# A gated recurrence on one core: two pairs of PSUM banks for the level products, the next keys prepared a level ahead, and a shorter norm chain

## What is computed

```python
def chunked_gated_recurrence(q, k, v, log_f):
    ...
    def step(state, inp):
        qc, kc, vc, lfc = inp
        b = jnp.cumsum(lfc, axis=2)
        ...
        scores = jnp.einsum('nhtk,nhsk,nhtsk->nhts', qc, kc, decay)
        o_intra = jnp.einsum('nhts,nhsv->nhtv', scores, vc)
        ...
def hgrn2_mixer(x, w_in, lower_bound, norm_g, w_out):
    q, f_fw, f_bw, i_in, g = jnp.split(x @ w_in, 5, axis=-1)
    ...
    o = o[:bsz] + flip(o[bsz:])
    o = rms_norm(o, norm_g)
    ...
    o = o * jax.nn.silu(g)
    return o @ w_out
```

## Time and profile before

| what | value |
| --- | --- |
| median of three runs | 2890.19 us (2887.98 to 2890.64) |
| profiled execution, its own time | 2895.3 us |
| its span in the profile | 2893.5 us |
| TensorE busy, share of the span | 2668.3 us, 92% |
| VectorE busy, share | 1422.0 us, 49% |
| ScalarE busy, share | 555.3 us, 19% |
| GpSimd busy, share | 618.9 us, 21% |
| mean granted TensorE clock | 0.959 of full speed |

### The profile page before, as it was taken

How to read it: one execution, slowest core, us unless ns; L and a number is a source line. 1 busy time by engine, 2 the same in 40 slices (tenths; PEclk the granted TensorE clock), 3 DMA queues, 4 the chain that set the end, 5 groups by cost and what they waited for, 6 DMA issues and landing times. The chain is left out here.

```text
span 2893.5 us, 35029 instructions
## 1 busy us (share of the span) xinstructions
PE 2668.3 (92%) x13476; PEld 2229.2 (77%) x13476; DVE 1422.0 (49%) x2579; ACT 555.3 (19%) x825; POOL 618.9 (21%) x448
## 2 busy tenths in 40 slices
PE   6786889999999999978999999995899999999996
PEld 5676678788888888767888888885778888888875
DVE  8699526523332232463666766666472232333227
ACT  3224232211111111012322222320211111111110
POOL 2969211111112111111111111100111111111210
PEclk8898899999999999989999999996999999999998
DMA  4333223121111111021011011100511112111101
GB/s 133 85 104 100 78 74 131 58 59 44 43 43 43 58 43 58 8 72 37 23 37 37 22 36 29 36 7 0 185 57 50 44 43 58 43 43 43 43 15 58
DMA packets 207701, 157.96 MB, mean 55 GB/s; under 512 B 15616, under 2 KB 189824, under 8 KB 206720
## 3 DMA queue, kind: packets, MB, share of 16 engines
q1 hardware_dynamic: 207616, 156.81, 17.8%
HBM read 139.02 MB, written 17.76 MB: 54 GB/s over the span
## 5 line engine op out<-in xcount | busy, mean ns | idle before, releaser
L588 DVE TENSOR_TENSOR h<-h,ps 128x512 f32<-128x512 f32 x320 | 219.6, 686 | 201.2 <-PE ps L365 200.9
L347 PE MATMUL ps<-aT_hi,w_hi 128*128 128x512 f32 x704 | 278.4, 395 | 3.2 <-DVE aT_lo L561 3.2
L347 PE MATMUL ps<-aT_hi,w_lo 128*128 128x512 f32 x704 | 276.6, 393 | 0.0
L347 PE MATMUL ps<-aT_lo,w_hi 128*128 128x512 f32 x704 | 274.4, 390 | 0.0
L1738 PE MATMUL ps<-aT_hi,w_hi 128*128 128x512 f32 x640 | 258.4, 404 | 1.7 <-PEq L241 1.7
L1738 PE MATMUL ps<-aT_hi,w_lo 128*128 128x512 f32 x640 | 251.6, 393 | 0.0
L1738 PE MATMUL ps<-aT_lo,w_hi 128*128 128x512 f32 x640 | 250.9, 392 | 0.0
L1710 POOL TENSOR_TENSOR w_lo<-w_raw,w_hi 128x1024 fp32r<-128x1024 f32 x38 | 93.0, 2454 | 578.2 <-ACT w_hi L62 578.2
L571 DVE TENSOR_TENSOR s5o_act_out<-s5o_act_out,ps 128x512 f32<-128x512 f32 x44 | 30.2, 687 | 351.5 <-ACT s5o_act_out L460 351.5
L571 DVE TENSOR_TENSOR hgo_act_out<-hgo_act_out,ps 128x512 f32<-128x512 f32 x44 | 30.2, 687 | 349.9 <-ACT hgo_act_out L460 349.9
L1771 PE MATMUL ps<-hg_q_decayed,hg_k_used 128*128 128x128 f32 x896 | 128.7, 302 | 34.7 <-DVE hg_scores L2062 31.9
(11 more groups left out here) (325 smaller groups left out, 5951.2 us busy)
## 6 DMA issues: line engine op xcount, KB each, us to landing
w_raw<-in_ffn_w_in_dram SPq DMA_DIRECT2D x44, 512.0 KB, 5.1
w_raw<-in_hg_w_in_dram SPq DMA_DIRECT2D x40, 512.0 KB, 3.9
s5o_raw<-in_ffn_w_in_dram SPq DMA_DIRECT2D x22, 512.0 KB, 5.0
s5o_raw<-in_ffn_w_out_dram SPq DMA_DIRECT2D x11, 1024.0 KB, 5.0
hgo_raw<-in_ffn_w_in_dram SPq DMA_DIRECT2D x22, 512.0 KB, 5.0
hgo_raw<-in_ffn_w_out_dram SPq DMA_DIRECT2D x11, 1024.0 KB, 5.0
h<-in_x_dram SPq DMA_DIRECT2D x4, 1024.0 KB, 9.0
s_w_raw<-in_s_w_in_dram SPq DMA_DIRECT2D x8, 512.0 KB, 4.9
```

The source lines that it names most:

```text
L347: ins = t.matmul(ps[:, 2 * b + a, :], w[q][:, a, kk, :], x[:, kk, rows], start=(kk == 0 and m == 0), stop=(kk == KT - 1 and m == 2))
L588: v.tensor_tensor(part, part, ps[:, 4 + m % 4, :], ALU.add).then_inc(S["out_acc"], 1)
```

## The change

It has five parts. Odd levels write banks 4 and 5 instead of 2 and 3, so a level waits for the scores of the level before the last (`level_kept` of `lv - 1`), and level 1 of a head waits for the former head's output to be out of banks 4 and 5 (`o_kept`) instead. `advance_k(n, lv)`, the step that brings k forward, now stands a level ahead: for level 0 of the next head it stands at the end of a head, behind `keep_g` ("behind the gate"), and for level `lv + 1` it stands behind the scores' copy of level `lv`. The diagonal scores are taken behind the q move of level 0 instead of ahead of everything. `turn_k` waits for level 5's scores instead of `o_kept`. The norm chain has three Newton steps of three operations instead of four of four, which makes 11 small operations with the mean instead of 18. With three Newton steps instead of four the inverse root is computed by a slightly different approximation.

```diff
--- before.py
+++ after.py
@@ -1629,7 +1629,7 @@
     OUTS = HG_OUTS
     BUF = [0, 1, 0, 1, 0]
     USES = [BUF.count(0), BUF.count(1)]
-    CORE = 2 * (NHC - 2) + 1 + RSQRT_STEPS
+    CORE = 2 * (NHC - 2) + 2 + 3 * NEWTON
     PREPARED = 2 * HLV + 2
 
     def first(n):
@@ -1766,16 +1766,18 @@
                         t.wait_ge(E["o_normed"], n)
                 if lv:
                     t.wait_ge(E["level_moved"], HLV * n + lv)
-                    t.wait_ge(E["level_kept"], HLV * n + lv)
+                if lv == 1 and not first(n):
+                    t.wait_ge(E["o_kept"], 2 * n)
+                if lv >= 2:
+                    t.wait_ge(E["level_kept"], HLV * n + lv - 1)
                 for c in range(NHC):
-                    ins = t.matmul(bank_rows(2)[:, c, :], k_used[lv % 2][:, c * HC:(c + 1) * HC], q_used(lv, c),
+                    ins = t.matmul(bank_rows(2 + 2 * (lv % 2))[:, c, :], k_used[lv % 2][:, c * HC:(c + 1) * HC], q_used(lv, c),
                                    start=True, stop=True)
                 ins.then_inc(E["level_done"], 1)
 
             def turn_k(n):
                 t.wait_ge(E["level_moved"], HLV * (n + 1))
-                if not first(n):
-                    t.wait_ge(E["o_kept"], 2 * n)
+                t.wait_ge(E["level_kept"], HLV * n + HLV - 1)
                 t.wait_ge(E["diag_kept"], n + 1)
                 for d in range(2):
                     for c in range(NHC):
@@ -2019,48 +2021,57 @@
                 for d in range(2):
                     v.tensor_tensor(Q[d][:, :], q_raw[:, :], f_raw[d][:, :], ALU.mult).then_inc(E["prepared"], 1)
 
+            def advance_k(n, lv):
+
+                now, then = k_used[lv % 2], k_used[1 - lv % 2]
+                if lv == HLV - 1:
+                    v.tensor_copy(halves(then, lv, 1), halves(k_other, lv, 1)).then_inc(E["k_passed"], 1)
+                else:
+                    passed = [a[:, :].rearrange("p (b e) -> p b e", e=4 << lv)[:, :, 1 << lv:3 << lv]
+                              for a in (then, k_other)]
+                    v.tensor_copy(*passed).then_inc(E["k_passed"], 1)
+                v.wait_ge(E["k_passed"], HLV * n + lv + 1)
+                carry(v, n)
+                for d in range(2):
+                    by = pair(d, lv, 1 - d)
+                    if lv == HLV - 1:
+                        v.tensor_tensor(halves(k_other if d else then, lv, d), halves(now, lv, d),
+                                        bc(by, 2, [P, NHC, 1 << lv]), ALU.mult)
+                    else:
+                        by = by.rearrange("p (b e) -> p b e", e=2)
+                        for e in range(2):
+                            v.tensor_tensor(quarter(then if d == e else k_other, lv, 2 * e + d),
+                                            quarter(now, lv, 2 * e + d),
+                                            bc(by[:, :, e], 2, [P, T // (4 << lv), 1 << lv]), ALU.mult)
+
             def core(n, more):
                 link = Steps(E["chain"], n * CORE)
                 v.wait_ge(E["prepared"], (n + 1) * PREPARED)
-                v.wait_ge(E["diag_done"], n + 1)
-                for b in range(2):
-                    ins = v.tensor_tensor(scores[:, 4 * b:4 * b + 4, :],
-                                          ps[:, 6 + b, :].rearrange("p (c t) -> p c t", t=HC),
-                                          bc(k.ident[:, :], 1, [P, 4, HC]), ALU.mult)
-                ins.then_inc(E["diag_kept"], 1)
-                v.wait_ge(E["diag_kept"], n + 1)
                 for lv in range(HLV):
-                    now, then = k_used[lv % 2], k_used[1 - lv % 2]
+                    v.wait_ge(E["level_done"], HLV * n + lv + 1)
+                    carry(v, n)
                     if not (first(n) and lv == 0):
                         v.wait_ge(E["level_moved"], HLV * n + lv)
                         carry(v, n)
-                    if lv == HLV - 1:
-                        v.tensor_copy(halves(then, lv, 1), halves(k_other, lv, 1)).then_inc(E["k_passed"], 1)
-                    else:
-                        passed = [a[:, :].rearrange("p (b e) -> p b e", e=4 << lv)[:, :, 1 << lv:3 << lv]
-                                  for a in (then, k_other)]
-                        v.tensor_copy(*passed).then_inc(E["k_passed"], 1)
-                    v.wait_ge(E["k_passed"], HLV * n + lv + 1)
-                    carry(v, n)
-                    for d in range(2):
-                        by = pair(d, lv, 1 - d)
-                        if lv == HLV - 1:
-                            v.tensor_tensor(halves(k_other if d else then, lv, d), halves(now, lv, d),
-                                            bc(by, 2, [P, NHC, 1 << lv]), ALU.mult)
-                        else:
-                            by = by.rearrange("p (b e) -> p b e", e=2)
-                            for e in range(2):
-                                v.tensor_tensor(quarter(then if d == e else k_other, lv, 2 * e + d),
-                                                quarter(now, lv, 2 * e + d),
-                                                bc(by[:, :, e], 2, [P, T // (4 << lv), 1 << lv]), ALU.mult)
-                    v.wait_ge(E["level_done"], HLV * n + lv + 1)
-                    carry(v, n)
                     for d in range(2):
                         qs = halves(Q[d], lv, 1 - d)
                         ins = v.tensor_tensor(qs, qs, bc(pair(d, lv, d), 2, [P, T // (2 << lv), 1 << lv]), ALU.mult)
                     ins.then_inc(E["level_moved"], 1)
-                    v.copy_predicated(scores[:, :, :], bc(mask[:, lv, :], 1, [P, NHC, HC]), bank_rows(2)
-                                      ).then_inc(E["level_kept"], 1)
+                    if lv == 0:
+                        v.wait_ge(E["diag_done"], n + 1)
+                        for b in range(2):
+                            ins = v.tensor_tensor(scores[:, 4 * b:4 * b + 4, :],
+                                                  ps[:, 6 + b, :].rearrange("p (c t) -> p c t", t=HC),
+                                                  bc(k.ident[:, :], 1, [P, 4, HC]), ALU.mult)
+                        ins.then_inc(E["diag_kept"], 1)
+                        v.wait_ge(E["diag_kept"], n + 1)
+                        carry(v, n)
+                    v.copy_predicated(scores[:, :, :], bc(mask[:, lv, :], 1, [P, NHC, HC]),
+                                      bank_rows(2 + 2 * (lv % 2))).then_inc(E["level_kept"], 1)
+                    if lv < HLV - 1:
+                        v.wait_ge(E["level_moved"], HLV * n + lv + 1)
+                        carry(v, n)
+                        advance_k(n, lv + 1)
                     if more and lv < 2:
                         keep_q(n + 1, lv)
 
@@ -2087,7 +2098,16 @@
                 v.wait_ge(E["o_squared"], NHC * (n + 1))
                 v.tensor_scalar(ms[:, :], ms[:, :], 1.0 / P, RMS_EPS, ALU.mult, ALU.add).then_inc(E["chain"], 1)
                 v.wait_ge(E["chain"], link.step())
-                rsqrt_steps(link, v, rs[:, :], rt[:, :], ms[:, :])
+                v.tensor_scalar(rs[:, :].bitcast(I32), ms[:, :].bitcast(I32), -0.5, 1597463007.0, ALU.mult, ALU.add
+                                ).then_inc(E["chain"], 1)
+                v.wait_ge(E["chain"], link.step())
+                for _ in range(NEWTON):
+                    v.tensor_tensor(rt[:, :], rs[:, :], rs[:, :], ALU.mult).then_inc(E["chain"], 1)
+                    v.wait_ge(E["chain"], link.step())
+                    v.scalar_tensor_tensor(rt[:, :], rt[:, :], -0.5, ms[:, :], ALU.mult, ALU.mult).then_inc(E["chain"], 1)
+                    v.wait_ge(E["chain"], link.step())
+                    v.scalar_tensor_tensor(rs[:, :], rt[:, :], 1.5, rs[:, :], ALU.add, ALU.mult).then_inc(E["chain"], 1)
+                    v.wait_ge(E["chain"], link.step())
                 for b in range(2):
                     ins = v.tensor_tensor(scores[:, 4 * b:4 * b + 4, :],
                                           ps[:, 2 + b, :].rearrange("p (c t) -> p c t", t=P),
@@ -2101,6 +2121,8 @@
                 if more:
                     for half in range(2):
                         keep_g(n + 1, half)
+                    v.wait_ge(E["init"], n + 2)
+                    advance_k(n + 1, 0)
                 assert link.n == CORE
 
             for half in range(2):
@@ -2109,6 +2131,8 @@
                 keep_g(0, half)
             prepare_totals(0)
             prepare_q(0)
+            v.wait_ge(E["init"], 1)
+            advance_k(0, 0)
             core(0, True)
             with v.Fori(1, HEADS - 1) as n:
                 core(n, True)
```

## The result

The changed kernel takes 2858.97 us (median of four runs, 2856.04 to 2860.54) against 2890.18 us for the kernel before (2887.98 to 2890.64). The ratio is 0.9889 (95% interval 0.9877 to 0.9902): 31.2 us faster, where 31.1 were forecast. The profiled execution took 2860.23 us, with a span of 2858.4 us.

The account below looks back on a forecast made before the run. TensorE was taken to bound the middle heads, with time winnable only where it stands still. Savings of 15.5 + 5.7 + 1.4 + 8.5 = 31.1 us from the median 2890.2 give 2859.1 us (-1.08%), range 2850 to 2870.

Parts of the forecast that it names:

- What a stall is worth: Each TensorE stall costs 0.25 us beyond its listed wait: 0.16 hidden idle time and about 0.09 for restarting.
- all thirteen of the levels' stalls: Two pairs of banks remove the scores-copy waits at levels 1 and 3 outside the last head: 15.5 us.
- five of the turning's: The shorter norm chain removes five of six TensorE waits before turning outputs: 4.6 us listed, 5.7 us in all.
- 81.7 us a head: Sign of being right: the middle heads lie 81.7 us apart instead of 85.3.
- Level 1's tight place: At head boundaries, level 1's q move arrives 0.1 us before it is wanted, so the stall goes without slack.
- three more operations held in turn: Feared at the boundary: GpSimd's subtractions (2.4 us each) hold k-step operations, making the q move 5 to 7 us late.
- The first rival: Level 1 of six heads keeps its 1.09 + 0.25 us stall: 8 us less gain, 2867 us; chance 0.13.
- the slower one: Rival: level 1 waits longer for the q move than for the copy; 11 us slower, 2901 us; chance 0.03.
- the 2.6 us of my step: In the last head, level 1 starts 2.6 us earlier, with diagonal operations and scores copy now behind it.
- The chain: Norm chain: eleven operations at 0.203 us take 2.24 us instead of 3.66; the last head gains 1.4 us in full.
- The last head: Its levels save 7.2 us at the low clock, 12.0 at the high; 8.5 us taken.
- VectorE's pace: In the last head at full clock, VectorE sets the distance of the levels at 4.3 us.

Follow-up runs that it names:

- e2: The kernel before with only the two pairs of banks and their waits, old order and old norm chain: 2866.53 us, ratio 0.9914.
- e1: The kernel before with only the shorter norm chain of three fused Newton steps: 2881.32 us, ratio 0.9967.
- e8: The kernel before once more, nothing edited, for a second profile: 2889.14 us, block 743.32 us.
- e3: The kernel before with the two pairs of banks and the short norm chain, in the old order of VectorE: 2863.70 us, ratio 0.9903.
- e7: The changed kernel once more, nothing edited, for a second profile: 2857.51 us, ratio 0.9882 against the kernel before.
- e6: The changed kernel with extra matmuls, read by nobody, where TensorE waits in head 7: 2853.46 us, ratio 0.9878 against the kernel before.
- e10: The changed kernel with e6's extra matmuls, and ScalarE taking the copy of each k step in head 7: 2849.88 us, ratio 0.9854 against the kernel before.
- e5: The changed kernel with the old norm chain of four Newton steps (18 small operations): 2869.47 us, ratio 0.9925 against the kernel before.
- e9: The changed kernel with a fourth fused Newton step in the norm chain: 2859.05 us, ratio 0.9884 against the kernel before.
- e4: The changed kernel with one pair of banks again, new order and short chain kept: 2887.76 us, ratio 0.9988 against the kernel before.
- e11: The same kernel as e6, run again beside e10: 2854.64 us, ratio 0.9868 against the kernel before.

## Why the prediction was right

*What a stall is worth, and all thirteen of the levels' stalls, with five of the turning's.* 15.5 + 5.7 = 21.2 us were forecast; heads 0 to 6 gave 1.2 + 19.9 = 21.1. e2 and e1 show that each part takes its own waits: 2.33 us of a middle head by the banks (85.28 to 82.95) and 1.01 by the chain, which makes 3.34, where both together gave 3.32. The turning's price, 0.92 + 0.22 = 1.14 us in five heads, was right: e1 gives 1.12 to 1.17 in each. Left out were the 0.3 us that heads 0 and 6 gain without a listed wait, 0.6 in all. The levels were priced too high by about as much: 2.50 us a head where e2 gives 2.33, so that a level's stall costs some 0.20 us beyond what is listed (14.0 us gained in heads 1 to 6 of e2, 11.6 listed in e8, twelve stalls) and not 0.25. That the two cancel is luck. The forecast of 81.7 us a head took the price of a head with all three stalls from a mean that includes head 6, which has only two; it is 81.95.

*Level 1's tight place.* The reckoning, a copy held by GpSimd until 0.29 us behind its subtractions, four free multiplications and a q move 0.1 us before it is wanted, came out within a tenth: 0.28, and 0.14 us. The Trainium skill, SBUF — State Buffer, "Who interferes with whom", says that the second to start is blocked on the shared port; the trace agrees for the copy (1.95 us against 0.43 in e3, where it comes at the end of GpSimd's work). What the rule made me fear, three more operations held in turn, did not happen, since the pair of subtractions had ended. The first rival (level 1 keeps its stall) and the slower one fall with that.

*What I credited to the order.* Nothing in the sum hung on it in the middle heads, but the text reads as if the place of the k step were needed there. e3 shows that it is not. It starts level 1 of head 7 1.2 us earlier; the other 1.3 of the 2.6 us of my step came from the banks, since in e3, too, level 1 no longer waits for the scores copy. The block of e7 is 3.7 us below e3's, but little of that can be put down to the order. 2.7 lie ahead of head 1: 1.35 before the first level 0, where e3's first 10 us ran at a granted clock of 0.85 and e7's at 1.00, and 1.4 in head 0, which takes 83.5 us in e6 and e10 too, and they have the new order. The other 1.0 lies in the levels of head 7, which scatter by as much (e5 and e9, with the new order and the same levels as e7, took 36.01 and 36.05 against 34.76). The medians of e3 and the changed kernel differ by 4.7 us, and their intervals (0.9888 to 0.9919, 0.9877 to 0.9902) overlap.

*The chain.* The fused operation on 128x8 was taken at 0.203 us and is 0.20 from start to start. The forecast chain of 2.24 us is 2.21. In the last head I gave it 1.4 us, and the wait ahead of the turning there shows just that: 8.22 or 8.23 us in the four kernels with the old chain (before, e8, e2, e5) and 6.78 to 6.80 in five with the new one (changed, e7, e1, e3, e4). The whole stretch behind the levels gains 1.5 us by e8 and e7, 1.6 by e1, but 0.9 by e3 against e2 and 0.2 by e7 against e5, since the work ahead of that wait scatters: from the turning of k to the first output 9.2 to 10.6 us, the outputs themselves 6.6 to 8.0, in instructions that these edits leave alone.

*The last head.* The term that was mis-sized most: 8.5 forecast, 10.1 measured (44.90 to 34.76). The frame was right, 7.2 at the low clock and 12.0 at the high. I took a value near the row with 0.51, but with the shorter stands (idle times of TensorE between two levels) the clock came back for part of the levels (0.71 in the window, two levels of 2.05 us among four of 3.04 to 3.78). e6 shows the cause: with nothing changed but added work on TensorE the clock is 0.95 and the levels lie 4.23 us apart, VectorE's pace (4.3 forecast). The Trainium skill, TensorE: Matmul & The Clock Gate, "What's actually happening", has activity release the throttled clock; the trace agrees, in part in the changed kernel (0.71) and fully in e10 (1.00). Against the block's 32.8 us the sum of 31.1 is short by 1.7, and 1.6 of that is this term. The two comparisons of medians give 31.2 and 33.0 us, so that the first meets the forecast within 0.1 is luck.

## What to carry to other kernels

Where two engines hand over through one buffer, ask which of the waits a second buffer removes and what is late next: here the second pair of banks was worth 24 us of 31, the shorter chain 7 to 8, and the rewritten order 1.2 us that can be located. An operation that reads PSUM can run in the time in which GpSimd works beside VectorE (the diagonal took its usual 1.28 us there in e3), while a copy from SBUF to SBUF is held (1.95 us in place of 0.43); so move the copy out of that time, if something useful can take its place, and count first, for here it was a draw. A stretch in which TensorE waits again and again is priced at both levels of its clock, and matmuls without a use in its gaps can pay: 4.5 us of the last head here, and another 3 of its levels once VectorE's share of the loop shrank as well. A mean over heads hides that one of them has fewer waits; compare head by head.

## What was unexpected of the hardware

In e4 a stand of 2.51 us between a unit and a level, in heads that are otherwise solid TensorE work, was followed by the low clock, but in every second head only: level 1 took 3.60 us with granted 0.51 in head 3 (3.61 and 3.58 us in heads 1 and 5), and 2.16 us with 1.00 in heads 2 and 4 (1.00 in head 6 too). They are the same instructions, with waits of 2.51 us in heads 2, 3 and 6 and 2.53 in heads 4 and 5 (2.14 in head 1). What decides between them no run shows. In the kernel before a stand of 1.09 us never did it in heads 1 to 6 (granted 1.00 over all). The clock's return scatters as well. Ahead of the diagonal of head 0 TensorE waits 7.9 us in eleven of the thirteen profiles (5.7 in the first of before and in e4), and the level that follows is shown, in e6 and then in e11, which are the same kernel, as:

```profile
1353.54 3.79 PE L1774 MATMUL ps<-hg_q_decayed,hg_k_used 128*128 128x128 f32 x16 [0.65 <-DVE hg_q_decayed L2035]
```

```profile
1357.03 2.92 PE L1774 MATMUL ps<-hg_q_decayed,hg_k_used 128*128 128x128 f32 x16 [1.05 <-DVE hg_q_decayed L2035]
```

Head 0 takes 83.55 us in the one and 81.98 in the other. The way to its first level scatters likewise, 68.3 to 68.4 us in ten profiles and 69.7 in three (before, e3, e5); in those three the first 10 us of the block ran at a granted clock of 0.85 or 0.86, in the others at 1.00. The levels of the last head scatter by 1.3 us (e5 and e9 against e7). A single profile of this kernel can therefore tell a part of under 3 us only where it stands in heads 1 to 6, or in a wait that is read by itself. Whether a given build falls into the one or the other more often than chance, which would explain the rest of the medians of e3 and e5, no run here settles.
